# A mixture-of-experts layer on one core: bias rows packed in DRAM, a PSUM bank for each unit, the first pass written out, gathers by units

## The chip, the cores and the metric

The kernel runs on one core of one Trainium2 chip. The metric is the device time of one execution in microseconds. The kernel before takes 2048.38 us (median of three runs, 2045.47 to 2049.39). The execution that the profiler recorded took 2049.03 us; its span, from the first instruction to the last, is 2047.3 us.

Engines are called by their names in the profile: PE (TensorE), DVE (VectorE), ACT (ScalarE), POOL (GpSimd), SP (SyncE). An engine that ends in q (SPq, DVEq) is that engine's sequencer, which works through registers, branches and waits and issues the DMAs.

## The reference

One transformer-like layer on 1024 tokens of 1024 channels in float32: a modulated norm, a recurrent and a gated branch, an output projection, and then a mixture of 32 experts of which each token takes four. The part that the change touches is the experts:

```python
def expert_block(args):
    xb, e = args
    gu = xb @ w_gu[e] + b_gu[e]            # 1024 -> 2048
    g, lin = jnp.split(gu, 2, axis=-1)
    g = jnp.minimum(g, SWIGLU_LIMIT)
    lin = jnp.clip(lin, -SWIGLU_LIMIT, SWIGLU_LIMIT)
    act = g * jax.nn.sigmoid(SWIGLU_ALPHA * g) * (lin + 1.0)
    return act @ w_down[e] + b_down[e]     # 1024 -> 1024
...
ys = ys.astype(jnp.float32) * row_gate[:, None]
out = jnp.zeros((n_tok + 1, d), jnp.float32).at[row_tok].add(ys)[:n_tok]
```

An expert's weights are 12 MB (8 MB for `w_gu`, 4 MB for `w_down`), its biases 12 KB.

## The kernel before, in words

The program is written engine by engine, in order, with semaphores between them; nothing reorders it. The first 440 us compute the dense part, the routing and the tables. The rest is the experts.

**Units and items.** A unit is 32 rows (tokens) of one expert. The rows of an expert are cut into items of one to four units. This input has 47 items and 143 units. Experts are taken in an order of places: a large one, then a small one, and so on. A matrix product on PE has 32 rows as its stationary side, and four column quarters of the weights go through four 32-column tiles of the array. So the output of a unit lies in one PSUM bank as 128 partitions x 512 columns (gate and linear part) or x 256 (down).

**One item on PE** (`down_of`, `gate_and_linear_of`): the loop is turned by one stage. An iteration does the down product of item g (`down`, L1359, 64 matmul instructions a unit) and then the gate and linear product of item g + 1 (`gate_and_linear`, L1339, 64 a unit, in two halves of four weight slabs). Units are taken from the highest number to 0 (`units_down`), by branches on the item's count. Between the two stand small products that make the list of rows of a later item (`make_list`, L1299, `repeat_rows`, L1311). `down` writes banks 4 and 5 in turn, and for units 0 and 1 waits on `dn_drained` until DVE has read the result of two units before.

**The same item on DVE**: `block_rows` (one transpose of all gathered rows of the next item, L1942), the tables for the items after it (`make_onehot` L1934, `rows_here`, `make_idx`, `make_gates`, up to L1823), then for each unit `activate` (bias, limits, product with the sigmoid of ACT, transpose; L1969 to L1984), the list (`read_list` L1802), and for each unit `result` (down bias and gate weight; L1991, L1994). In front stand reads of words of the item's table into registers (L424). The loop body has this order for every item, the first one too.

**ACT** applies the norm's scale and shift to the transposed rows (`modulate`, L964) and the sigmoid (L974). **POOL** gathers the rows of an item by index (`gather`, L722; always four indirect DMAs, whatever the item's count) and adds results into an accumulator in DRAM (`scatter`, L733, one a unit). Both are 128 x 256 floats, in rows of 1 KB.

**SP** loads the weights in twelve chunks of 1 MB (L524). The buffers hold one expert, so chunk q of the next expert is issued when PE has used chunk q of this one for the last time (`freed[q]`). Between chunk 7 (the last of `w_gu`) and chunk 8 (the first of `w_down`) come the biases (`bias_in_rows`): eight DMAs, which copy the expert's biases to all 32 rows of each of four partition groups, in runs of 1 KB.

**The first item** has a pass of its own on PE (`first_1a` and so on), since its row tables are made at the same time; then the loops begin. SP, DVE, ACT and POOL enter their loops with item 0.

## Time and profile before

| | |
|---|---|
| median of three runs | 2048.38 us |
| the profiled execution, its span | 2049.03 us, 2047.3 us |
| PE busy | 1940.1 us, 95% of the span |
| DVE, POOL, ACT busy | 48%, 25%, 17% |
| DMA | 527.37 MB, 258 GB/s on average |
| mean granted TensorE clock | 0.983 |
| experts: PE's first gate product to its last down product | 445 to 2026 us |

Busy shares say which engine works most, not who waits for whom. The rows that follow the prediction's steps are in the section before it: each has its start in us from the span's start, its length, engine, source line, operation, and in square brackets the idle time of the engine before it and what ended it. The granted clock is in shares of 2.4 GHz: 1.00 is that level, 0.50 is 1.2 GHz, and a value between them is a stretch with both.

### The profile page before, as it was taken

Reading aid. Unit: us, or ns where it says so; the run is one execution under the profiler, and the core shown is the slowest. Engines: PE = TensorE matmul, PEld = TensorE weight load, DVE = VectorE, ACT = ScalarE, POOL = GpSimd, SP = SyncE. Lnnn points to the kernel's source line nnn. Section 1 sums busy time; section 2 is a strip of 40 time slices with the busy share of each in tenths; the row PEclk is TensorE's granted clock in tenths of the full one; section 3 lists DMA queues with packets and bytes.
Section 4 is the critical chain, followed back from the end, with each engine's and each line's share of the span. In section 5 each row is a group of like instructions: output and inputs, shape, how many; then the busy total and the mean of one; then the engine's idle time right before and its main releaser. Section 6 shows DMA issues by size and latency. Waiting matters only on the chain.

```text
span 2047.3 us, 53441 instructions
## 1 busy us (share of the span) xinstructions
PE 1940.1 (95%) x20292; PEld 812.1 (40%) x20293; DVE 989.9 (48%) x2301; ACT 356.0 (17%) x740; POOL 502.4 (25%) x540
## 2 busy tenths in 40 slices
PE   5999989968999999999999999999999999999996
PEld 3444444523333333334343443344334443334432
DVE  4666545354534445454444444454444454444435
ACT  4243121230100101111111111111111111111003
POOL 1100022133222222323232322323223222322221
PEclk9999999989999999999999999999999999999998
DMA  9333317341871964959595979879798898999995
GB/s 375 91 136 123 123 36 215 120 180 35 292 267 26 334 225 136 381 175 367 177 364 198 387 262 370 298 287 397 278 390 290 300 390 281 393 402 346 320 340 196
DMA packets 125697, 527.37 MB, mean 258 GB/s; under 512 B 17248, under 2 KB 47600, under 8 KB 75472
## 3 DMA queue, kind: packets, MB, share of 16 engines
q1 hardware_dynamic: 92272, 470.46, 58.9%
q0 software_dynamic: 33184, 56.29, 11.8%
q8 instruction: 20, 0.33, 0.1%
q14 instruction: 29, 0.24, 0.0%
q10 hardware_dynamic: 192, 0.06, 0.0%
HBM read 494.35 MB, written 32.38 MB: 257 GB/s over the span
## 4 chain that ended last, share of the span: by engine, by line
PE 81%; DMA 10%; DVE 3%; issue 2%; ACT 1%; SPq 1%; POOL 1%; DVEq 0%; another core or an unknown queue 0%; ACTq 0%; POOLq 0%
PE psum L1339 42%; PE psum L1359 20%; PE psum L1081 8%; DMA big<-in_exp_w_down_dram 6%; PE psum L1255 5%; DMA big<-in_exp_w_gu_dram 3%; PE psum L1192 2%; PE psum L1124 1%; PE psum L1299 0%; PE psum L1096 0%; SPq L524 0%; PE psum L1311 0%; DMA big<-in_w_out_dram 0%; PE psum L1106 0%
## 5 line engine op out<-in xcount | busy, mean ns | idle before, releaser
L1339 PE MATMUL psum<-big,r 128*32 128x512 f32 x9152 | 1001.8, 596 | 17.9 <-DMA big<-in_exp_w_gu_dram 9.0
L1339 PEld LDWEIGHTS psum<-big,r 128*32 128x32 f32 x9152 | 292.9, 110 | 680.0 <-issue 657.6
L1359 PE MATMUL psum<-big,r 128*32 128x256 f32 x9152 | 519.4, 383 | 25.6 <-DVE r L1984 16.9
L733 POOL DMA_INDIRECT acc_rows<-r,scatter_idx x139 | 220.5, 1586 | 778.6 <-DVE r L1994 746.5
L1359 PEld LDWEIGHTS psum<-big,r 128*32 128x32 f32 x9152 | 303.5, 111 | 220.9 <-DVE r L1984 22.7
L964 ACT ACTIVATE r<-r,shift 128x128 f32<-128x128 f32 x368 | 150.9, 480 | 883.2 <-PE psum L1339 698.4
L1969 DVE TENSOR_TENSOR r<-psum,r 128x256 f32<-128x256 f32 x143 | 59.1, 413 | 344.8 <-PE psum L1339 258.1
L722 POOL DMA_INDIRECT r<-hs_rows,gather_idx x188 | 185.8, 988 | 83.3 <-issue 43.1
L1991 DVE TENSOR_TENSOR r<-psum,r 128x256 f32<-128x256 f32 x143 | 60.7, 425 | 272.6 <-PE psum L1359 254.7
L1081 PE MATMUL psum<-r,big 128*128 128x512 f32 x384 | 166.3, 593 | 1.6 <-ACT r L853 1.6
L1942 DVE STREAM_TRANSPOSE r<-r 128x1024 f32<-128x1024 f32 x46 | 96.0, 2087 | 105.8 <-issue 105.8
L974 ACT ACTIVATE r<-r 128x256 f32<-128x256 f32 x143 | 59.6, 417 | 465.0 <-DVE r L1975 444.0
L1255 PE MATMUL psum<-big,r 128*128 128x512 f32 x256 | 112.2, 594 | 0.7 <-DMA big<-in_w_out_dram 0.5
L1081 PEld LDWEIGHTS psum<-r,big 128*128 128x128 f32 x384 | 72.6, 190 | 91.6 <-issue 89.2
L1984 DVE STREAM_TRANSPOSE r<-r 128x256 f32<-128x256 f32 x143 | 93.3, 653 | 4.9
L1980 DVE TENSOR_TENSOR r<-r 128x256 f32<-128x256 f32 x143 | 60.9, 426 | 49.9 <-ACT r L974 49.2
L1994 DVE SCALAR_TENSOR_TENSOR r<-r,g1row,g_rows 128x256 f32<-128x256 f32 x143 | 69.3, 485 | 5.1
L1255 PEld LDWEIGHTS psum<-big,r 128*128 128x128 f32 x256 | 47.8, 190 | 59.2 <-issue 57.8
L719 POOL COPY gather_idx<-r 128x4 int32 (+1 forms) x47 | 8.7, 186 | 249.8 <-DVE r L1816 249.8
L1934 DVE TENSOR_TENSOR r<-r 128x1024 bf16<-128x1024 f32 (+1 forms) x49 | 60.0, 1226 | 7.1 <-DVE r L1932 1.5
L1982 DVE TENSOR_TENSOR r<-r 128x256 f32<-128x256 f32 x143 | 60.8, 425 | 4.9
L1971 DVE SCALAR_TENSOR_TENSOR r<-psum,r 128x256 f32<-128x256 f32 x143 | 59.3, 415 | 0.0
(316 smaller groups left out, 938.4 us busy)
## 6 DMA issues: line engine op xcount, KB each, us to landing
big<-in_exp_w_gu_dram SPq DMA_DIRECT2D x256, 1024.0 KB
big<-in_exp_w_down_dram SPq DMA_DIRECT2D x128, 1024.0 KB
big<-in_ada_w_dram SPq DMA_DIRECT2D x12, 2048.0 KB, 13.8
r<-in_x_dram SPq DMA_DIRECT2D x16, 512.0 KB, 8.7
big<-in_w_in_dram SPq DMA_DIRECT2D x4, 2048.0 KB, 19.5
r<-in_exp_b_gu_dram SPq DMA_DIRECT2D x128, 64.0 KB
big<-in_w_out_dram SPq DMA_DIRECT2D x2, 2048.0 KB, 12.7
hs_rows<-r POOLq DMA_DIRECT2D x8, 512.0 KB, 3.0
```

Source lines behind the costliest of these rows:

```text
L722: pool.indirect_dma_start(z_quarters[:, u, :], None, hs_quarters, bass.IndirectOffsetOnAxis(ap=gather_idx[:, u:u + 1], axis=0)).then_inc(r ...
L733: pool.indirect_dma_start(acc_quarters, bass.IndirectOffsetOnAxis(ap=scatter_idx[:, u:u + 1], axis=0), y_sb[:, u, :], None, bounds_check=4 ...
L964: ins_ = act.activation(izT[:, k, :].rearrange("p (u n) -> p u n", u=UMAX), z_blocks[:, :, k, :], ACT.Identity, bias=shift2[:, 1, k:k + 1] ...
L1081: last = pe.matmul(b, w[:, k, m * P:(m + 1) * P], zT[:, k, th * 512:(th + 1) * 512], start=(k == 0), stop=(k == KT - 1))
L1255: last = pe.matmul(b, src[:, ct % CT, t * P:(t + 1) * P], ring(("wout", dh))[:, ct, :], start=(ct == 0), stop=(ct == 2 * CT - 1))
L1339: last = pe.matmul(psum[32 * j:32 * j + 32, u, :].rearrange("p (a n) -> p a n", a=2), izT[:, k, u * UNIT:(u + 1) * UNIT], rhs[:, :, 256 * ...
L1359: ins_ = pe.matmul(psum[32 * i:32 * i + 32, 4 + u % 2 if bank is None else bank, 0:256], actT[:, u, f, :], down_slab(f)[:, 256 * i:256 * i ...
L1942: dve.transpose(z_blocks, z_quarters.rearrange("p u (n k) -> p u k n", k=KT)).then_inc(z_blocked, 1)
L1980: dve.tensor_tensor(gsig_sb[:, u % 2, :], gate_u, sig_sb[:, u % 2, :], ALU.mult).then_inc(gsig_made, 1)
L1982: dve.tensor_tensor(act_sb[:, u % 2, :], lin_u, gsig_sb[:, u % 2, :], ALU.mult).then_inc(act_made, 1)
L1984: dve.transpose(actT[:, u, :, :], act_sb[:, u % 2, :].rearrange("p (n k) -> p k n", k=KT)).then_inc(at_made, 1)
L1994: dve.scalar_tensor_tensor(out=y_sb[:, u, :], in0=y_sb[:, u, :], scalar=gate_cur[:, u:u + 1], in1=g2_rows[:, :], op0=ALU.mult, op1=ALU.mul ...
```

## The change

It has four parts.

1. **Biases packed.** At the start POOL copies the biases of all experts with three DMAs from DRAM to DRAM into `bias_pack`, in which the 768 values that one partition group needs lie together. An expert's biases are then four DMAs with runs of 3 KB in place of eight with runs of 1 KB.
2. **A bank for each unit.** `down` writes bank 4 for unit 0 and bank u for unit u (the one that held its gate and linear part). Now the next item's gate product of unit u > 0 waits until that bank is drained (`results_of[u]`), unit 0's down product waits for all results of the item before, and PE computes four registers an item for that.
3. **The first pass written out.** Item 0 leaves the loops of DVE and ACT. DVE makes the table of item 3, activates item 0 and only then does `block_rows(1)` and the rest; ACT does item 0's sigmoids before it modulates item 1.
4. **Gathers by units.** POOL gathers only the units that an item has, and counts them in a register. DVE counts the same ahead of each `block_rows`: one more word read, up to three branches, up to four additions.

```diff
+            for a, (name, at) in enumerate((("exp_b_gu", 0), ("exp_b_gu", D), ("exp_b_down", 0))):
+                pool.dma_start(bias_pack[:, :, 256 * a:256 * a + 256],
+                               ins[name][0, :, at:at + D].rearrange("e (j n) -> e j n", j=4)).then_inc(bias_packed, SEMW)
...
                 for j in range(4):
-                    rows = bias_rows[32 * j:32 * j + 32, at:at + BIAS]
-                    sp_.dma_start(rows[:, 0:512].rearrange("p (a n) -> p a n", a=2),
-                                  ins["exp_b_gu"][0, bass.ds(e, 1), :].rearrange("o (a n) -> o a n", a=2)
-                                  [:, :, 256 * j:256 * j + 256].broadcast_to([UNIT, 2, 256])).then_inc(bias_in, SEMW)
-                    sp_.dma_start(rows[:, 512:768],
-                                  ins["exp_b_down"][0, bass.ds(e, 1), 256 * j:256 * j + 256].broadcast_to([UNIT, 256])
-                                  ).then_inc(bias_in, SEMW)
+                    sp_.dma_start(bias_rows[32 * j:32 * j + 32, at:at + BIAS],
+                                  bias_pack[bass.ds(e, 1), j, :].broadcast_to([UNIT, BIAS])).then_inc(bias_in, SEMW)
...
-                for u in range(UMAX):
-                    pool.indirect_dma_start(z_quarters[:, u, :], None, hs_quarters,
-                                            bass.IndirectOffsetOnAxis(ap=gather_idx[:, u:u + 1], axis=0)
-                                            ).then_inc(rows_in, SEMW)
+                units_down(pool, wanted, gather_unit)
...
+            units_down(act, act.to_reg(item_value(act, IT_UNITS, 0, 1, UMAX)), sigmoid)
+            act.wait_ge(freed[3], 1)
+            modulate(1, 0)
+            act.wait_ge(freed[7], 1)
+            modulate(1, 1)
             last_item = act.snap(total - 1)
-            with act.Fori(0, last_item) as g:
+            with act.Fori(1, last_item) as g:
...
+            def results_to_wait_for():
+
+                for u in range(UMAX):
+                    pe.reg_add(results_of[u], downs, SPARE - u)
...
+                    if k == 0 and u > 0 and steady:
+                        pe.wait_ge(dn_drained, results_of[u])
...
-                if u < 2 and bank is None:
-                    pe.wait_ge(dn_drained, downs)
+                if u == 0:
+                    pe.wait_ge(dn_drained, results_of[0])
...
-                        ins_ = pe.matmul(psum[32 * i:32 * i + 32, 4 + u % 2 if bank is None else bank, 0:256],
+                        ins_ = pe.matmul(psum[32 * i:32 * i + 32, DOWN_BANK[u], 0:256],
...
             with pe.Fori(0, last_item) as g:
                 down_of(g)
                 begin_item()
+                results_to_wait_for()
                 gate_and_linear_of(g + 1)
...
             def block_rows(turn):
 
-                dve.wait_ge(rows_in, turn * (UMAX * SEMW))
+                units_down(dve, dve.to_reg(item_value(dve, IT_UNITS, turn, 1, UMAX)),
+                           lambda u: dve.reg_add(rows_due, rows_due, SEMW))
+                dve.wait_ge(rows_in, rows_due)
...
-            with dve.Fori(0, last_item) as g:
+            make_onehot(3, link)
+            units, prior, place, bias_at = item_words(0)
+            activate_all(units, place, bias_at)
+            block_rows(1)
+            rows_here(4, link)
+            make_idx(2, link)
+            make_gates(2, link)
+            read_list(5)
+            link(dve.tensor_copy(gate_cur, gate_of[:, 0:UMAX]))
+            dve.wait_ge(acc_out, prior * SEMW + SEMW * TT)
+            dve.sem_inc(may_start, 1)
+            units_down(dve, units, lambda u: result(u, bias_at, DOWN_BANK[u]))
+            base = chain[0]
+            with dve.Fori(1, last_item) as g:
...
-                units_down(dve, units, lambda u: result(u, bias_at, 4 + u % 2))
+                units_down(dve, units, lambda u: result(u, bias_at, DOWN_BANK[u]))
```

What stands in DVE's program at the start of item 0, where the loop began before. TENSOR_LOAD at L424 is the read of a word of the item's table (L426 in the changed kernel), and L1942 the transpose of the next item's rows. Before:

```order
L2003 TENSOR_SCALAR r<-r 128x72
L2020 UNCONDITIONAL_BRANCH
L2020 ISA
L424 TENSOR_LOAD r
L424 ISA x3
L424 TENSOR_LOAD r
L424 ISA x3
L424 TENSOR_LOAD r
L424 ISA x2
L1939 ISA
L1942 STREAM_TRANSPOSE r<-r 128x1024
```

And in the changed kernel at the same place (L2029 is the old L2003, L1943 to L1956 make the table of item 3, L2042 is the wait for the biases):

```order
L2029 TENSOR_SCALAR r<-r 128x72
L426 TENSOR_LOAD r
L426 ISA x2
L426 TENSOR_LOAD r
L426 ISA x2
L1943 ISA
L1943 COPY g1row<-r 128x48
L1954 ISA
L1954 TENSOR_TENSOR r<-r 128x128
L1956 ISA
L1956 TENSOR_TENSOR r<-r 128x1024
L426 TENSOR_LOAD r
```

The transpose has gone from here, and with it one word read before the table; the transpose now follows the last unit's activation.

DVE in the loop of the changed kernel, after the fourth word read and ahead of the transpose (L1968, the old L1942); these rows are new:

```order
L433 COMPARE_AND_BRANCH
L433 UNCONDITIONAL_BRANCH
L433 COMPARE_AND_BRANCH
L433 UNCONDITIONAL_BRANCH
L433 COMPARE_AND_BRANCH
L433 UNCONDITIONAL_BRANCH
L1964 REGISTER_ALU
L435 UNCONDITIONAL_BRANCH
L1964 REGISTER_ALU
L435 UNCONDITIONAL_BRANCH
L1964 REGISTER_ALU
L435 UNCONDITIONAL_BRANCH
```

They are branches on the next item's count and additions to `rows_due`; they stand between the result of one item's unit 0 and the transpose.

## Rows read from the trace of the kernel before

**Rows 1.** The page's chain that ended last, by engine.
```profile
PE 81%; DMA 10%; DVE 3%; issue 2%; ACT 1%; SPq 1%; POOL 1%; DVEq 0%; another core or an unknown queue 0%; ACTq 0%; POOLq 0%
```
**Rows 2.** Waits of PE from 520 us on: in total, times, longest.
```profile
PE psum L1359 <- DVE r L1984: 11.8, 11, 4.9
PE psum L1339 <- DMA big<-in_exp_w_gu_dram: 9.0, 8, 2.7
...
PE psum L1359 <- DMA big<-in_exp_w_down_dram: 4.3, 6, 1.4
```
**Rows 3.** Timeline of PE, first item into second.
```profile
490.56 8.50 PE L1359 MATMUL psum<-big,r 128*32 128x256 f32 x128 [5.16 <-DVE r L1984]
501.10 7.11 PE L1359 MATMUL psum<-big,r 128*32 128x256 f32 x128 [2.04 <-issue]
508.14 0.25 PE L1311 MATMUL psum<-g1row,r 128*128 128x6 bf16 x4
508.33 7.07 PE L1339 MATMUL psum<-big,r 128*32 128x512 f32 x64
```
**Rows 4.** Timeline of DVE, first item.
```profile
481.22 2.07 DVE L1942 STREAM_TRANSPOSE r<-r 128x1024 f32<-128x1024 f32 x1 [2.52 <-issue]
...
483.69 1.22 DVE L1934 TENSOR_TENSOR r<-r 128x1024 bf16<-128x1024 f32 x1 [0.15 <-DVE r L1932]
...
487.44 0.42 DVE L1969 TENSOR_TENSOR r<-psum,r 128x256 f32<-128x256 f32 x1 [1.14 <-issue]
...
489.87 0.64 DVE L1984 STREAM_TRANSPOSE r<-r 128x256 f32<-128x256 f32 x1
...
498.76 0.65 DVE L1984 STREAM_TRANSPOSE r<-r 128x256 f32<-128x256 f32 x1
...
500.57 0.42 DVE L1991 TENSOR_TENSOR r<-psum,r 128x256 f32<-128x256 f32 x1 [1.05 <-issue]
```
**Rows 5.** Chain, first item: DVE's sequencer at word reads, then at branches.
```profile
478.92 0.32 DVEq L424
...
479.57 0.07 DVEq L424
...
486.54 0.08 DVEq L431
...
487.15 0.04 DVEq L1966
```
**Rows 6.** PE in a stretch: length, busy, granted clock, DMA share, GB/s.
```profile
490.00:495.00 5.00, 4.44 (x56) 0.66 0.31 84
```
**Rows 7.** Timeline of PE: the longest weight stall at each of three experts.
```profile
1174.60 7.93 PE L1339 MATMUL psum<-big,r 128*32 128x512 f32 x72 [1.79 <-issue]
...
1266.89 9.63 PE L1339 MATMUL psum<-big,r 128*32 128x512 f32 x72 [2.72 <-DMA big<-in_exp_w_gu_dram]
...
1453.43 7.98 PE L1359 MATMUL psum<-big,r 128*32 128x256 f32 x144 [1.37 <-DMA big<-in_exp_w_down_dram]
```
**Rows 8.** DMA queues at 691.9:694.5, then 469:480: packets, MB, share of 16 engines.
```profile
q1 hardware_dynamic: 537, 0.47, 60.5%
...
q0 software_dynamic: 192, 0.52, 15.9%
```
**Rows 9.** A stretch with weights alone: length, POOL busy, clock, DMA share, GB/s.
```profile
973.00:978.00 5.00, 0.00 (x0) 1.00 1.02 405
```
**Rows 10.** Timeline of SP: first bias issue of an expert, and first w_down issue.
```profile
1245.00 0.34 SPq L531 DMA_DIRECT2D r<-in_exp_b_gu_dram  x1
...
1250.09 9.92 SPq L524 DMA_DIRECT2D big<-in_exp_w_down_dram  x4
```
**Rows 11.** Timeline of DVE in a two-unit item.
```profile
1049.11 0.16 DVE L1823 TENSOR_TENSOR r<-g1row 128x4 f32 x1
1051.48 0.43 DVE L1969 TENSOR_TENSOR r<-psum,r 128x256 f32<-128x256 f32 x1 [2.20 <-PE psum L1339]
```
**Rows 12.** Timeline of PE: unit 0's down product in the same item.
```profile
1059.42 3.66 PE L1359 MATMUL psum<-big,r 128*32 128x256 f32 x64 [0.18 <-DVE r L1984]
```

More of the change, by code:

```diff
@@ L70 @@
 BIAS = 768
+BIAS_LOADS = 4
 LISTS = MAX_ITEMS + 3
@@ L567, in _ @@
                     if q == 7:
-                        sp_.wait_ge(bias_in, SEMW * 8 * place)
+                        sp_.wait_ge(bias_in, SEMW * BIAS_LOADS * place)
                         if place >= 2:
@@ L1321, in _ @@
             downs = counter(pe, "downs")
-            all_drained = pe.alloc_register("all_drained")
+            results_of = [counter(pe, f"results_of{u}") for u in range(UMAX)]
+            def results_to_wait_for():
+                for u in range(UMAX):
+                    pe.reg_add(results_of[u], downs, SPARE - u)
+            results_to_wait_for()
             def load_word(turn, i):
@@ L1331, in begin_item, with gate_and_linear @@
                 pe.reg_add(arrived, arrived, SEMW)
-            def gate_and_linear(u, half, first=False, between=None):
+            def gate_and_linear(u, half, first=False, between=None, steady=False):
                 for k in range(4 * half, 4 * half + 4):
@@ L1347, in gate_and_linear, with down @@
                     last.then_inc(gu_made, 1)
-            def down(u, bank=None):
+            def down(u, last=False):
                 pe.reg_add(downs, downs, 1)
                 pe.wait_ge(at_made, downs)
-                if u < 2 and bank is None:
-                    pe.wait_ge(dn_drained, downs)
+                if u == 0:
+                    pe.wait_ge(dn_drained, results_of[0])
                 for f in range(KT):
@@ L1358, in down @@
                     for i in range(4):
-                        ins_ = pe.matmul(psum[32 * i:32 * i + 32, 4 + u % 2 if bank is None else bank, 0:256],
+                        ins_ = pe.matmul(psum[32 * i:32 * i + 32, DOWN_BANK[u], 0:256],
                                          actT[:, u, f, :], down_slab(f)[:, 256 * i:256 * i + 256],
                                          start=(f == 0), stop=(f == KT - 1), skip_group_check=True)
-                    if u == 0 and f in (1, 3, 5) and bank is None:
+                    if u == 0 and f in (1, 3, 5) and not last:
                         ins_.then_inc(freed[8 + f // 2], 1)
@@ L1442, in gate_and_linear_of @@
                 pe.wait_ge(z_made[0], g + 1)
-                units_down(pe, units, lambda u: gate_and_linear(u, 0))
+                units_down(pe, units, lambda u: gate_and_linear(u, 0, steady=True))
                 pe.wait_ge(z_made[1], g + 1)
@@ L1466, in _ @@
             spread = counter(pe, "spread")
-            pe.reg_add(all_drained, downs, SPARE)
-            pe.wait_ge(dn_drained, all_drained)
-            units_down(pe, units, lambda u: down(u, DOWN_BANK[u]))
+            units_down(pe, units, lambda u: down(u, last=True))
             units_down(pe, units, spread_sum)
@@ L2049, in last_step @@
                 ins_.then_inc(dve_chain, 1)
-                dve.wait_ge(dve_chain, loops + (base + count_[0]))
+                dve.wait_ge(dve_chain, loops + (base - STEPS + count_[0]))
             units, prior, place, bias_at = item_words(last_item)
```

21 lines of the change are left out of this document (16 added, 5 removed).

## The prediction, as recorded before the changed kernel ran

> **What bounds the kernel now.** I read the chain that ended last, then PE's waits, then timelines where PE stands still. PE holds 81% of the chain and DMA 10% [rows 1]. So time can be won only where PE waits, or be lost where PE gets a new wait. From 520 us on PE waits little: 11.8 us for DVE, 9.0 and 4.3 us for weights [rows 2]; with 1.8 us that the profile calls issue in the middle of a gate product [rows 7] the weight stalls are 15.1 us. In a four-unit item nothing is left to win: the small list product is followed by the next gate product with no idle time [rows 3]. The largest single hole lies in the first item. PE waits 5.16 us for DVE, runs two units' down products in 8.50 us, waits another 2.04 us, and runs the other two in 7.11 us [rows 3]. The second wait is the bank: unit 1 needs unit 3's result, and DVE does that result, at 500.57, only after all four activations [rows 4]. The first two units are slower by 1.4 us since the granted clock is 0.66 after the wait, a mix of 2.4 and 1.2 GHz, against 1.00 later [rows 6].
>
> **First pass and banks.** Before, DVE reads three words, transposes item 1's rows for 2.07 us from 481.22, reads two more words, makes the table of item 3 (1.22 us from 483.69) and starts to activate at 487.44 [rows 4]. A word costs 0.65 us, the time between two reads in the chain, and the first read begins at 478.92 [rows 5]. After, in steps:
> - two reads end at 480.2; the table starts 0.4 us later, as it did behind the transpose, and is done at 481.8;
> - three reads run beside it and end near 482.7; three branches take 0.61 us (486.54 to 487.15 [rows 5]) and the first instruction comes 0.3 us after them [rows 4]: activation starts at 483.6, its transpose ends 3.1 us later (487.44 to 490.51 [rows 4]), at 486.7;
> - PE starts unit 3's down product at about 486.8 in place of 490.56. Units are activated every 2.96 us (489.87 to 498.76 for three [rows 4]), a down product takes 3.5 us, so it then never waits. I let the clock fall again, as it did after the wait of 5.16 us, and keep the 1.4 us. End of four units: 486.8 + 14.1 + 1.4 = 502.3;
> - with a bank per unit the 2.04 us wait goes. What is late next is the first gate product of item 1, which now wants unit 3's result. DVE: last activation ends 495.6, one read and the branches and additions 1.6, transpose 2.07, tables 1.6 (484.91 to 486.54 [rows 4, 5]), list and copy 0.2, on to the result 1.05 + 0.42 [rows 4], so 502.6. ACT needs 1.65 us behind the transpose (499.3) and is earlier.
> So item 1 starts at about 502.8 and not 508.33 [rows 3]: -5.5 us. Bounds: -3.7 if only the start moves and another wait takes the place of the 2.04; -7.2 if clock and result cost nothing. In the other items the bank change removes nothing, as no wait on it shows in PE's list, and adds a wait only on results that are several units old.
>
> **Weight stalls.** They come where a small item, or an item that is an expert's only one, gives the next 12 MB too little time. By the unit counts of the timeline (matmul count over 64) there are eight such places. Their stalls: 1.7 at 572 us, 2.7 at 720, 1.0 at 852, 4.1 at 1162 to 1188, 3.4 at 1254 to 1267, 1.7 at 1451 to 1453, 0.2 and 0.4 later (the longest of three of them in [rows 7]). There the DMA engines are full, so what counts is their time. An expert's biases are 384 KB in 1 KB runs. In the stretch where they dominate SP's queue, 0.47 MB take 60.5% of 2.6 us, 1.57 us [rows 8], so 0.39 MB take 1.31 us; at the weights' 405 GB/s [rows 9] they would take 0.97. Packed: -0.34 us an expert. Bounds: 0, and the whole 1.31. A gather that isn't made saves 15.9% of 11 us over four, 0.44 us [rows 8]. Before the stalls at 1162, 1254 and 1451 three unit gathers go (items of two and three units ahead): 0.34 + 3 x 0.44 = 1.66 each, 5.0 together. The biases lie behind the `w_gu` chunks in SP's order, so the first three stalls gain only by gathers: none, one (0.44), none. The last two, 0.6, vanish. Sum -6.1 us. Gathers and packing elsewhere are worth nothing.
>
> The Trainium skill (DMA: Bandwidth & Descriptors, section Bandwidth) says that transfers under 64 KB are bound by their descriptors and gives 0.95 us of DMA time for 64 KB. By that, eight pieces against four would be worth some 2.6 us an expert, an estimate from that page, and the sum would be about 4 us lower; the 1.57 us for all of 0.47 MB in this trace speaks against it.
>
> **What the loops gain in work.** DVE's count of gathered rows stands between the last result and the transpose, where DVE is idle for the sequencer already: a read 0.65, three branches 0.61 [rows 5], additions and jumps about 0.3 at 0.04 to 0.1 each (L1966 [rows 5]): 1.6 us an item, estimated. Behind it on DVE wait the table and all activations, and PE waits for these. In items of three and four units DVE idles several us before the first activation. In the 11 two-unit items it idles 2.20 us, of which 1.0 is its branches [rows 11, 4]: cover 1.2, so the activation is 0.4 late. PE waits 0.18 us at unit 0 already [rows 12], so 0.22 us an item; three of them run into a weight stall that hides it: 8 x 0.22 = +1.8 us. The two one-unit items pay the full 1.6 (PE's 4.9 us wait [rows 2] becomes 6.5), but the stalls of 1.7 and 2.7 us behind them take it up: 0. Bounds: 0 to 11 x 1.6 = 18. I stay near the low end because the cover is a row.
>
> The Trainium skill (Advanced Engine Details and Errata, Control Flow Timing) gives about 108 ns for a compare-and-branch and 51 ns for a plain branch. By these the activation would be hardly late and the sum 1.8 us lower; the trace has 0.20 us for each of three branches on DVE, and goes first.
>
> POOL's branches are hidden, since POOL (25% busy) waits for DVE ahead of every scatter. The packing runs some 200 us before the first bias is wanted, so SP's wait for it is long met. PE's four register additions and its waits stand at a place where four register operations and three branches leave no gap [rows 3]: 0.
>
> **Sum.** -5.5 - 6.1 + 1.8 = -9.8 us. The profiled execution took 2049.03 us (span 2047.3, 1.7 around it), 0.65 above the median of the runs. 2049.0 - 9.8 = 2039.2 us.
>
> **Rivals.**
> - *A, the stalls stay.* The weights alone need 12.6 MB / 405 GB/s = 31 us an expert, and a three-unit item lasts 31.7. If the engines lose the saved time elsewhere, only the first pass counts: -5.5 + 1.8, 2045.3 us. For it: the chain's DMA pieces of 24 to 27 us. Against: gathers show a plain share of engine time.
> - *B, SP's issues are the limit.* Bias issues fill 5.09 us ahead of `w_down` [rows 10]; halved, `w_down` starts 2.5 us sooner. With 1.3 for gathers that clears up to 3.9 at 1162, and 3.4 and 1.7 whole, with 0.44 and 0.6: -10.0, so 2035.3 us. Against: the engines are full in that stretch, so an earlier issue only queues.
> - *C, the first pass gains little*, as a late word read or code fetch on DVE holds it: -1.5, with the rest 2043.2 us. The 1.05 and 1.14 us gaps [rows 4] show how dear DVE's sequencer is.
> - *D, slower.* PE's sequencer has no lead at the item boundary, and four additions, 0.09 us each on DVE with the gap before them [rows 5], stand open: 0.36 x 46 = +16.6 us, 2055.8 us. It is slower than before from 0.21 us an item. Against: the gap between L1311 and L1339 is zero now [rows 3].
>
> **Chances.** Forecast 0.55, A 0.17, B 0.12, C 0.07, D 0.09. Range 2032 to 2050 us: it takes in A, B, C and the bounds of the first pass, and half of the open cost on DVE, and leaves out D. A measurement tells 0.2% (4.1 us) from no change, so faster means below 2044.3: forecast and B nearly whole, most of C, a third of A: 0.76. Same 0.14. Slower 0.10.
>
> **What would show it.** First unit's down product near 486.8 and item 1's first gate product near 502.8, with no wait between units 2 and 1. Weight stalls of about 9 us in place of 15.1. DVE's idle time before the block transpose up from 2.3 to about 3.9 us; PE's wait at unit 0 of two-unit items up from 0.18 to about 0.4. No gap between L1311 and the next gate product. I am wrong if that gap opens, if two-unit items lose more than 0.5 us, or if the stalls are as long as before.

## The result, and the profile after

The changed kernel takes 2027.74 us (median of 4 runs, 2026.08 to 2030.74), the kernel before 2046.93 (median of 4, one run more than above). The ratio is 0.9911, 95% interval 0.9895 to 0.9927: 18 to 19 us faster, where 9.8 us were forecast. The direction was right; the forecast gain is about half of the measured one, and the time lies below the forecast's range of 2032 to 2050 us.

PE's waits of the changed kernel from 520 us on (in total, times, longest):

```profile
PE psum L1362 <- DMA big<-in_exp_w_gu_dram: 10.2, 8, 2.2
PE psum L1382 <- DVE r L2010: 9.8, 2, 4.9
PE psum L1487 <- ACT r L1034: 6.4, 4, 3.9
PE psum L1313 <- DVE r L1956: 3.3, 2, 1.7
PE psum L1382 <- DMA big<-in_exp_w_down_dram: 3.3, 5, 1.4
```

Beside [rows 2] this is a riddle: 13.5 us for weights, against 15.1 before, and the kernel is 18 us faster. The first item, timeline of PE (start, length, operation, idle time before):

```profile
486.59 0.22 PE L1421 MATMUL psum<-ident_b 128*1 128x8 bf16 x3
486.74 0.35 PE L1313 MATMUL psum<-g1row,r 128*128 128x6 bf16 x8
490.37 15.71 PE L1382 MATMUL psum<-big,r 128*32 128x256 f32 x256 [3.28 <-DVE r L2010]
506.01 0.25 PE L1325 MATMUL psum<-g1row,r 128*128 128x6 bf16 x4
506.20 6.22 PE L1362 MATMUL psum<-big,r 128*32 128x512 f32 x56
```

A repeat product is the small product of `repeat_rows` (L1311 before, L1325 now) that closes an item's down products; the signals are the three small products at L1421 (L1398 before), right behind the first pass. Everything up to the signals lies 3.8 us later in this execution, and of the change only the packing of the biases has run by then. The last repeat product ahead of the signals began between 479 and 486 us in the profiles of all kernels here, with packing and without it, in no order, so distances count. From the three signals (L1421) to item 1's first gate product it is 19.61 us, against 25.51 before (482.82 to 508.33, [rows 3]): -5.9, forecast -5.5. The wait between units 2 and 1 is gone, and the gate product follows the repeat product without a gap, so rival D falls.

Then a two-unit item. The first two fences are PE in the kernel before, and DVE in the same place; the third is PE in the changed kernel:

```profile
840.55 0.35 PE L1299 MATMUL psum<-g1row,r 128*128 128x6 bf16 x8
840.84 0.64 PE L1359 MATMUL psum<-big,r 128*32 128x256 f32 x8
841.76 3.28 PE L1359 MATMUL psum<-big,r 128*32 128x256 f32 x56 [0.28 <-issue]
845.23 3.66 PE L1359 MATMUL psum<-big,r 128*32 128x256 f32 x64 [0.19 <-DVE r L1984]
848.82 0.26 PE L1311 MATMUL psum<-g1row,r 128*128 128x6 bf16 x4
```

```profile
840.00 0.65 DVE L1984 STREAM_TRANSPOSE r<-r 128x256 f32<-128x256 f32 x1
842.09 0.42 DVE L1969 TENSOR_TENSOR r<-psum,r 128x256 f32<-128x256 f32 x1 [1.43 <-PE psum L1339]
```

```profile
834.52 0.35 PE L1313 MATMUL psum<-g1row,r 128*128 128x6 bf16 x8
834.81 7.11 PE L1382 MATMUL psum<-big,r 128*32 128x256 f32 x128
841.85 0.26 PE L1325 MATMUL psum<-g1row,r 128*128 128x6 bf16 x4
```

In this execution of the kernel before, PE had finished unit 0's gate product by about 840.6 us and DVE was free too, but DVE began on it only at 842.09, after 1.4 us of idle time. The item took some 1.0 us more, and so it was in all eleven two-unit items: 11.5 us. I call it the hole. It looks like the missing half of the gain, since the changed kernel's profile has none. It isn't, as the experiments show.

### The profile page after: what moved, and what is told of

The parts are those of the page before. It is cut to its first block, busy times and chain, and to the rows that moved or that the text cites. A ratio compares the mean times of both kernels' runs of the same rounds, so it can differ in the third digit from the quotient of the medians.

```text
span 2028.9 us, 54052 instructions
## 1 busy us (share of the span) xinstructions
PE 1929.8 (95%) x20292; PEld 802.2 (40%) x20293; DVE 993.3 (49%) x2301; ACT 356.2 (18%) x740; POOL 463.3 (23%) x498
## 4 chain that ended last, share of the span: by engine, by line
PE 85%; DMA 10%; DVE 2%; ACT 1%; issue 1%; POOL 1%; DVEq 0%; ACTq 0%; SPq 0%; POOLq 0%
PE psum L1362 42%; PE psum L1382 23%; PE psum L1095 8%; DMA big<-in_exp_w_down_dram 6%; PE psum L1269 5%; DMA big<-in_exp_w_gu_dram 3%; PE psum L1206 2%; PE psum L1138 1%; PE psum L1313 1%; PE psum L1110 0%; PE psum L1325 0%; DVE r L2114 0%; DMA big<-in_w_out_dram 0%; PE psum L1120 0%; PE psum L1224 0%
## 5 line engine op out<-in xcount | busy, mean ns | idle before, releaser
L1362 PEld LDWEIGHTS psum<-big,r 128*32 128x32 f32 x9152 | 291.6, 110 | 677.2 <-issue 652.9
L1382 PE MATMUL psum<-big,r 128*32 128x256 f32 x9152 | 509.9, 382 | 16.3 <-DVE r L2010 13.1
L1382 PEld LDWEIGHTS psum<-big,r 128*32 128x32 f32 x9152 | 293.7, 111 | 211.9 <-DVE r L2010 13.3
L1968 DVE STREAM_TRANSPOSE r<-r 128x1024 f32<-128x1024 f32 x46 | 95.9, 2086 | 170.6 <-issue 170.6
L731 POOL DMA_INDIRECT r<-hs_rows,gather_idx x143 | 142.7, 998 | 123.6 <-issue 123.6
L1956 DVE TENSOR_TENSOR r<-r 128x1024 bf16<-128x1024 f32 (+1 forms) x49 | 60.0, 1225 | 7.1 <-DVE r L1954 0.9
## 6 DMA issues: line engine op xcount, KB each, us to landing
big<-in_exp_w_gu_dram SPq DMA_DIRECT2D x256, 1024.0 KB, 11.7
```

Source lines behind the costliest of these rows:

```text
L731: pool.indirect_dma_start(z_quarters[:, u, :], None, hs_quarters, bass.IndirectOffsetOnAxis(ap=gather_idx[:, u:u + 1], axis=0)).then_inc(r ...
L1362: last = pe.matmul(psum[32 * j:32 * j + 32, u, :].rearrange("p (a n) -> p a n", a=2), izT[:, k, u * UNIT:(u + 1) * UNIT], rhs[:, :, 256 * ...
L1382: ins_ = pe.matmul(psum[32 * i:32 * i + 32, DOWN_BANK[u], 0:256], actT[:, u, f, :], down_slab(f)[:, 256 * i:256 * i + 256], start=(f == 0) ...
L1968: dve.transpose(z_blocks, z_quarters.rearrange("p u (n k) -> p u k n", k=KT)).then_inc(z_blocked, 1)
```

## The experiments

Each ratio is against the kernel before on the same chip; the groups of runs came from several chips, so kernels of different groups are best compared by their ratios. Beside the times I use one measure: the time from one item's repeat product to the next is 42.03, 31.71 or 21.39 us for an item of four, three or two units where nothing waits; what is above that is the item's stall. The first item is counted from the last repeat product ahead of the signals. The three stall columns start at 842 us; the one-unit items at 550 and 697 us and the items behind them are not in them. The profile shows one execution and the time is the median of several, so the two need not agree (the profiled execution of "banks, first pass" was the slowest of its eleven). Each run gave one profile, so a row's stalls scatter by some 2 us, at 1150 and 1240 us by more.

| kernel | median us | ratio (95%) | first item | stalls at 842 | 1150 and 1240 | from 1300 |
|---|---|---|---|---|---|---|
| before, three profiles | 2045 to 2047 | 1 | 29.0, 28.8, 28.8 | 1.2, 1.9, 1.2 | 10.7, 11.0, 15.7 | 3.4 (with 11.5 of holes), 10.4, 9.8 |
| banks only | 2043.9 | 0.9991 (0.9981 to 1.0002) | 26.8 | 1.3 | 13.1 | 10.0 |
| first pass only | 2047.5 | 1.0004 (0.9994 to 1.0014) | 29.9 | 3.1 | 11.0 | 10.5 |
| banks, first pass | 2041.8 | 0.9974 (0.9963 to 0.9986) | 23.0 | 3.0 | 14.0 | 11.8 |
| changed, one wait more | 2029.0 | 0.9912 (0.9899 to 0.9925) | 23.0 | 1.7 | 10.6 | 2.2 |
| changed, down(1) in bank 5 | 2026.7 | 0.9905 (0.9890 to 0.9919) | 23.0 | 2.0 | 9.6 | 0.0 |
| packed biases only | 2043.2 | 0.9991 (0.9983 to 1.0000) | 28.8 | 2.1 | 12.2 | 5.8 |
| gathers by units only | 2038.9 | 0.9968 (0.9955 to 0.9980) | 30.7 | 2.3 | 11.2 | 3.9 |
| packed, gathers | 2037.7 | 0.9952 (0.9939 to 0.9966) | 30.7 | 1.8 | 11.8 | 2.4 |
| changed, gathers back | 2037.8 | 0.9964 (0.9952 to 0.9977) | 23.0 | 3.0 | 11.7 | 7.4 |
| changed, biases back | 2030.2 | 0.9922 (0.9909 to 0.9935) | 23.1 | 2.0 | 9.8 | 3.3 |
| changed, two profiles | 2027.7 | 0.9911 (0.9895 to 0.9927) | 23.1, 23.1 | 2.4, 1.9 | 10.7, 8.5 | 1.4, 1.0 |
| changed, biases ahead, two buffers | 2037.3 | 0.9963 (0.9949 to 0.9977) | 23.0 | 5.9 | 8.9 | 0.4 |
| changed, biases ahead, three buffers | 2039.5 | 0.9971 (0.9958 to 0.9983) | 23.1 | 6.3 | 7.9 | 0.1 |
| before, made hole | 2048.7 | 1.0014 (1.0006 to 1.0023) | 28.7 | 1.6 | 8.3 | 0.4 |
| changed, made hole | 2040.4 | 0.9975 (0.9965 to 0.9985) | 23.1 | 0.0 | 6.2 | 0.0 |
| changed, no bias loads | 2019.2 | 0.9874 (0.9859 to 0.9889) | 23.1 | 0.8 | 1.0 | 0.1 |

**1. Banks only.**

```
-        SPARE = 2
+        SPARE = 3
...
+                    if k == 0 and u > 0 and steady:
+                        pe.wait_ge(dn_drained, results_of[u])
...
-                if u < 2 and bank is None:
-                    pe.wait_ge(dn_drained, downs)
+                if u == 0:
+                    pe.wait_ge(dn_drained, results_of[0])
...
+                        ins_ = pe.matmul(psum[32 * i:32 * i + 32, DOWN_BANK[u], 0:256],
```

> The kernel before with one part of the change: a bank of its own for each unit's down product, and with it TensorE's waits on dn_drained moved (before at down(1) and down(0), now at gate(1..3) of the next item and at down(0)). Theory W (in the eleven two-unit items the first down product carries the wait on dn_drained before, and that is why DVE sees gu_made of unit 0 some 1.2 us late and down(0) starts late; the bank part alone removes it): 0.93 us x 11 = 10 us less, some of it given back to later weights, 2037 to 2040; the rows of a two-unit item show down x128 in one piece and DVE's first step of unit 0 right behind the transpose of unit 1. Rival G (the four gathers on GpSimd at that moment delay the signal, so it is the gathers by units that removed it): no change, 2045 to 2048, and the row with 1.43 us of idle time on DVE stays. The prediction on record gave this part 0.

No change clear of noise (0.9991, 0.9981 to 1.0002). The hole was gone, as theory W wants, and the gathers were not touched, against rival G. But the time, 2043.9 us, didn't follow into W's 2037 to 2040. Runs 8 and 12 below show that the kernel before mostly has no hole either, so its absence here decides neither.

**2 and 3. One wait more at down(1); down(1) in bank 5.** In the changed kernel:

```
-                if u == 0:
-                    pe.wait_ge(dn_drained, results_of[0])
+                if u == 0 or u == 1 and not last:
+                    pe.wait_ge(dn_drained, results_of[u])
```

> The changed kernel with one wait more: down(1) of every item also waits on dn_drained, for a count that gate(1) has waited for already, so that it never has to wait; banks as changed. Theory W (the instruction with the wait is what delays): the loss of the two-unit items comes back, 8 to 10 us, 2036 to 2038, with DVE idle 1.4 us before its first step of unit 0. Rival P (the PSUM bank: before, down(1) wrote bank 5, now bank 1): nothing comes back, 2027 to 2029.

```
-        DOWN_BANK = (4, 1, 2, 3)
-        SUM_BANK = (5, 6, 7, 0)
+        DOWN_BANK = (4, 5, 2, 3)
+        SUM_BANK = (1, 6, 7, 0)
```

> The changed kernel with down(1) in bank 5, as before, and the waits as changed. Rival P: the two-unit items lose their 0.93 us again, 2036 to 2038. Theory W: 2027 to 2029, and down x128 in one piece.

2029.0 us (0.9912, 0.9899 to 0.9925) and 2026.7 (0.9905, 0.9890 to 0.9919), two-unit items of 21.40 us in both. Neither the wait nor the bank brought the hole back, against W and P; with runs 8 and 12, where the kernel before has both the wait and the bank and no hole, neither is enough to make it.

**4. First pass only.** ACT's and DVE's share of item 0 ahead of their loops, activation first:

```
+            make_onehot(3, link)
+            units, prior, place, bias_at = item_words(0)
+            activate_all(units, place, bias_at)
+            block_rows(1)
...
-            with dve.Fori(0, last_item) as g:
+            with dve.Fori(1, last_item) as g:
```

> The kernel before with one part of the change: the first pass of DVE and ACT written out (activation of item 0 ahead of the block transpose, modulation ahead of the loop). By the prediction's first term the gate product of item 1 starts 5.5 us nearer to the first signal (25.5 us before, some 19.6 now): 2041 to 2042. If later weight stalls swallow a part, 2043 to 2044; the stalls from 1150 to 1270 us then grow by that.

No gain at all, and a miss of mine. PE in that kernel's first item:

```profile
487.73 8.80 PE L1364 MATMUL psum<-big,r 128*32 128x256 f32 x128 [3.23 <-DVE r L1989]
501.51 8.80 PE L1364 MATMUL psum<-big,r 128*32 128x256 f32 x128 [4.98 <-issue]
```

The first wait is 3.23 in place of 5.16 us [rows 3], but units 1 and 0 now wait 4.98 us in place of 2.04. The profile names no releaser for that wait; by the program it is their bank, since the results that free it stand behind block transpose and tables as before, and run 9 bears this out: with a bank for each unit the wait is gone. The first item is 1.1 us longer.

**5 to 7. Packed biases only; gathers by units only; both.**

```
-                    rows = bias_rows[32 * j:32 * j + 32, at:at + BIAS]
-                    sp_.dma_start(rows[:, 0:512].rearrange("p (a n) -> p a n", a=2),
...
-                    sp_.dma_start(rows[:, 512:768],
...
+                    sp_.dma_start(bias_rows[32 * j:32 * j + 32, at:at + BIAS],
+                                  bias_pack[bass.ds(e, 1), j, :].broadcast_to([UNIT, BIAS])).then_inc(bias_in, SEMW)
...
+            for a, (name, at) in enumerate((("exp_b_gu", 0), ("exp_b_gu", D), ("exp_b_down", 0))):
+                pool.dma_start(bias_pack[:, :, 256 * a:256 * a + 256],
...
```

> The kernel before with the biases packed in DRAM and loaded in four pieces, and nothing else of the change. The two runs with the bank part and the first pass part alone changed no time: both lost the 0.93 us hole of the two-unit items and paid it back in weight stalls (20.5 and 21.6 us against 15.1). Theory S (from 1150 us on the weights' arrival sets the time, and the eight bias DMAs between chunk 7 and chunk 8 are what holds it up): the stalls fall to 2 to 6 us, and the time to 2031 to 2038, lowest if the hole in the two-unit items goes as well. Theory of the record (packing is worth 0.34 us an expert, at the stalled experts alone): 2045 to 2046. Rival T (it is the gathers that hold the weights up): 2045 to 2048.

```
-                for u in range(UMAX):
-                    pool.indirect_dma_start(z_quarters[:, u, :], None, hs_quarters,
...
+                units_down(pool, wanted, gather_unit)
...
-                dve.wait_ge(rows_in, turn * (UMAX * SEMW))
+                units_down(dve, dve.to_reg(item_value(dve, IT_UNITS, turn, 1, UMAX)),
+                           lambda u: dve.reg_add(rows_due, rows_due, SEMW))
+                dve.wait_ge(rows_in, rows_due)
```

> The kernel before with gathers for the units of an item only, and DVE's count of them, and nothing else. Theory of the record: up to 5 us less stall at 1162 to 1454 us, 1.8 us more on DVE in two-unit items, so 2043 to 2045. Theory S: the stalls hardly change, 2045 to 2049. Rival T: 2034 to 2040.

> The kernel before with packed biases and gathers by units, without the banks and without the written-out first pass. Theory S: the supply is now free, what is left to the other two parts is the first pass, 5 to 6 us of the 19: 2032 to 2034. If the parts simply add, it is 2028, since banks and first pass alone gave nothing.

By the ratios, packing alone gave 1.8 us, at the edge of noise (theory S, which wanted 8 or more from it, falls in this form; the other two had 2045 or more, and it was 2043.2); the gathers alone 6.5, which only T had in its range; both 9.8 (2037.7 us, where S had 2032 to 2034 and the plain sum 2028, so both were missed). In the table the last column goes from 10 us to 5.8, 3.9 and 2.4. The gathers also have a price: DVE's count makes the first item 1.95 us longer, open on the path.

**8 and 12. The kernel before again, unchanged.**

> The kernel before, unchanged, for a second profile. If the hole of 0.28 us in the down product and DVE's 1.4 us before the last activation in two-unit items belong to the program (where its code lies, say), they are in this profile as well, 22.3 to 22.7 us for such an item; if they belong to one execution, the items take 21.4 us here.

> The kernel before, unchanged, a third profile, for how often the hole of the two-unit items comes: 22.4 us an item if it is there, 21.4 if not. The time should be some 5 us higher with it.

The hole is in neither: 21.39 us for each of the 22 two-unit items. They took 2043.54 and 2047.73 us, the execution with the holes 2049.03. So it belongs to an execution. The one-unit items at 550 and 697 us with their successors took 128.9 us in the execution with the holes and 125.4 and 125.0 in the other two, which is in no column of the table. PE's waits from 520 us on in the second one:

```profile
PE psum L1339 <- DMA big<-in_exp_w_gu_dram: 14.0, 10, 2.4
...
PE psum L1359 <- DMA big<-in_exp_w_down_dram: 8.9, 8, 1.4
```

22.9 us for weights, where the profile shown had 15.1. One of the late stalls in it, where the execution shown has a short wait only:

```profile
1681.22 0.25 PE L1311 MATMUL psum<-g1row,r 128*128 128x6 bf16 x4
1681.40 13.08 PE L1339 MATMUL psum<-big,r 128*32 128x512 f32 x120
1694.87 7.93 PE L1339 MATMUL psum<-big,r 128*32 128x512 f32 x72 [0.38 <-DMA big<-in_exp_w_gu_dram]
1702.74 0.35 PE L1299 MATMUL psum<-g1row,r 128*128 128x6 bf16 x8
1703.02 1.93 PE L1359 MATMUL psum<-big,r 128*32 128x256 f32 x32
1705.44 1.07 PE L1359 MATMUL psum<-big,r 128*32 128x256 f32 x16 [0.48 <-DMA big<-in_exp_w_down_dram]
1707.87 7.98 PE L1359 MATMUL psum<-big,r 128*32 128x256 f32 x144 [1.36 <-DMA big<-in_exp_w_down_dram]
1715.78 0.26 PE L1311 MATMUL psum<-g1row,r 128*128 128x6 bf16 x4
```

From 1681.22 to 1715.78 it is 34.56 us, 2.85 over 31.71. There are five such items from 1300 us on. Each is the first item of an expert whose weights are loaded during the only item, of three units, of the expert before it; at 1150 and 1240 us that only item has two units.

**9. Banks and first pass together** (the diffs of 1 and 4).

> The kernel before with the banks and the written-out first pass together, biases and gathers as before. Apart they took 2.0 us out of the first item (28.75 to 26.75 us from one repeat product to the next) and put 1.1 us in (29.89). Theory I (they work only together: a unit activated early waits for the bank, a free bank waits for the activation): some 22.9 to 23.1 us here, 5.8 less, and nothing of it lost later, since a weight stall is local to its expert: 2039 to 2042. Theory S' (the weights' arrival holds the end fixed, so any time won ahead of 1150 us goes into stalls): 2044 to 2047, with stalls 4 to 6 us longer.

Theory I holds for the first item, 23.0 us, and for the time, 5.3 us faster (0.9974, so 2.9 to 7.6) and outside the range of S'. But in this one profile, of the slowest of eleven executions, the three stall columns have 28.8 us, 3.8 more than the mean of the second and third profile before, where S' had 4 to 6. So that nothing is lost later is not shown.

**10 and 13. Biases an expert ahead.** Their DMAs behind the last `w_down` chunk of the expert before, with two buffers and with three:

```
...
-                    if q == 7:
...
-                        bias_in_rows(e, place)
+                if place + 1 < NE:
+                    bias_ahead(place + 1)
```

> The changed kernel with the bias DMAs of the next expert issued behind the last w_down chunk, an expert ahead, in place of between chunk 7 and chunk 8. Theory D (the DMA engines' time is what the stalled experts lack: the 0.39 MB leave the full stretch, some 1 us at each of eight stalls, where biases of the next expert take their place only in a stretch that is not full): 3 to 7 us less stall, 2021 to 2025. Theory Q (SP's issues, 2 us of them ahead of w_down, are what is lacking): the wait for w_down, 3.3 us in 5, goes and the wait for w_gu stays, 2024 to 2026. If neither: 2027 to 2029.

> The changed kernel with the biases an expert ahead, as in the run before, but with a third buffer for them, so that SP doesn't wait for the results of the expert just finished. With two buffers the late stalls (from 1300 us) were 0.3 us in place of 1.4 and the wait for w_down 0.6 in place of 3.3, but w_gu waits of 1.3 to 5.9 us came at 845, 957 and 1064 us. If SP standing at dn_drained ahead of chunk 0 made these: they go, 2022 to 2026. If the four bias issues and the word reads ahead of chunk 0 are enough to make them (some 3 us): 2032 to 2038 again.

Both slower than the changed kernel: 2037.3 us (0.9963, 0.9949 to 0.9977) and 2039.5 (0.9971, 0.9958 to 0.9983). The third buffer didn't help, so SP's wait for results is not the cause. In both the stalls from 1300 us are nearly gone (0.4 us with two buffers), but that at 842 us grew from 2.4 to 5.9 and 6.3, and four-unit items near 955 and 1062 us, which never waited, wait 0.9 to 1.8 us. PE at 842 us with three buffers:

```profile
844.93 1.07 PE L1368 MATMUL psum<-big,r 128*32 128x512 f32 x8 [0.62 <-DMA big<-in_exp_w_gu_dram]
847.22 1.90 PE L1368 MATMUL psum<-big,r 128*32 128x512 f32 x8 [1.22 <-DMA big<-in_exp_w_gu_dram]
850.27 20.13 PE L1368 MATMUL psum<-big,r 128*32 128x512 f32 x168 [1.15 <-DMA big<-in_exp_w_gu_dram]
```

The bias loads now lie ahead of `w_gu`, which PE wants first. With two buffers the profiled execution is 7.1 us longer than that of the changed kernel, and the items account for 6.8 of it: 3.3 us more at the one-unit items and behind them, 3.5 at 842 us, 2.8 near 955 and 1062, less 1.8 at 1150 and 1240 and 1.0 from 1300. Why a load there costs so much more than between chunk 7 and chunk 8 was not settled.

**11 and 15. The changed kernel with the gathers back, or with the biases back.**

> The changed kernel with all four gathers for every item again, and so without DVE's count: banks, first pass and packed biases stay. From the gathers part alone (2038.9 against 2045.7, stalls behind 5.9 us shorter, first item 1.95 us longer): with the first pass written out its count costs nothing there, so it should be worth more here: 2034 to 2036 without it. If parts add as ratios: 2034.

> The changed kernel with the biases in eight DMAs with rows of 1 KB again: banks, first pass and gathers by units stay. From bias packing alone (1.8 us) and on top of the gathers (3.3 us): 2030 to 2032 without it. The forecast's price of 0.34 us at the stalled experts: 2028.5 to 2029.5. Late stalls up from 1.4 to 3 or 4 us.

2037.8 and 2030.2 us: on top of the other parts the gathers are worth 10 us (the ratios say 11) and packing 2.4. The intervals of the ratios with and without packing overlap (0.9895 to 0.9927 and 0.9909 to 0.9935), so packing's share of the time is not clear of noise; the late stalls, 3.3 us without it and 1.4 and 1.0 with it, point the same way. The gathers' range was missed, they are worth more than I wrote.

**14 and 17. A hole made on purpose, in the kernel before and in the changed one.**

```
+            def hole():
+
+                pe.wait_ge(w_arrived[8], arrived)
+                for i in range(2):
+                    for j in range(4):
+                        pe.matmul(psum[32 * j:32 * j + 32, 3, :], down_slab(1)[:, 0:UNIT], down_slab(0)[:, 0:512],
+                                  start=True, stop=True, skip_group_check=True)
...
```

(in two-unit items only, ahead of down(1); bank 5 in the changed kernel)

> The kernel before, with eight matrix products of 128 x 512 (0.88 us) that nothing needs, ahead of the down products of each two-unit item: the hole that one of three profiles of it had, made on purpose, 11 x 0.9 = 9.7 us of TensorE. Theory S (the weights set the pace in the last part: a hole there only shortens the stall behind it): late stalls 10 us to 3 or 4, and the time only 1 to 4 us up, 2046 to 2049. Theory PE (TensorE's time adds to the end): 2054 to 2056.

> The changed kernel with the same useless products as in the run before last group's hole: eight in the program, which the trace of that run shows as sixteen of 1.74 us together, in each of eleven two-unit items, 19 us of TensorE in all. In the kernel before they cost 3 us. Theory S: the changed kernel has 1.3 us of late stalls left and 11 to 14 at three places further ahead (842, 1150, 1240 us), each behind one two-unit item, so it can hide 1.3 + 3 x 1.7 = 6 us of the 19: 2039 to 2042. If the changed kernel still were held by the weights: 2029 to 2032.

In the kernel before (L1453 is the hole):

```profile
1301.28 0.35 PE L1299 MATMUL psum<-g1row,r 128*128 128x6 bf16 x8
1301.57 1.92 PE L1453 MATMUL psum<-big 128*32 128x512 f32 x16
1303.31 7.09 PE L1359 MATMUL psum<-big,r 128*32 128x256 f32 x128
```

The eight products came out as sixteen, 1.74 us (1301.57 to 1303.31), twice what I had meant: 19 us of TensorE in all. They cost 2.9 us (1.0014, 1.0006 to 1.0023), within theory S and far from theory PE, which with 19 us would have had some 2065. The stalls from 1300 us fell from 10 to 0.4, those at 1150 and 1240 to 8.3. In the changed kernel the same products cost 12.7 us (2040.4 us), inside the range that was expected. The three stall columns fell to 6.2 us, from 14.5 and 11.4. Its waits for weights were then:

```profile
PE psum L1362 <- DMA big<-in_exp_w_gu_dram: 4.3, 4, 1.7
...
PE psum L1382 <- DMA big<-in_exp_w_down_dram: 2.3, 2, 1.3
```

**16. The changed kernel again.**

> The changed kernel, unchanged, for a second profile: its late stalls 0 to 2.5 us, those at 1150 and 1240 us 9 to 11 us together, as in its first profile and its two near copies, against 10 us and 11 to 16 us in the second and third profile of the kernel before.

2027.81 us, stalls 1.9, 8.5 and 1.0. A little under the range at 1150 and 1240.

**18. The changed kernel without bias loads from the third expert on** (it leaves out this part of the computation; its sums use stale biases).

```
-                        bias_in_rows(e, place)
+                        if place < 2:
+                            bias_in_rows(e, place)
+                        else:
+                            sp_.sem_inc(bias_in, SEMW * BIAS_LOADS)
```

> The changed kernel without the bias loads from the third expert on (the sums then use stale biases, so this part of the computation is left out): 29 x 0.39 MB that the DMA engines don't move and 4 issues less an expert on SP. Theory D (engine time, 1 us an expert, in the full stretches): late stalls 1.3 to 0, those at 842, 1150 and 1240 us 3 us shorter together, 2023 to 2025. Theory O (what counts in the queue is only what lies ahead of w_gu, and the biases lie behind it): only the wait for w_down goes, 3 us, 2024 to 2026. If biases are free where they are: 2027 to 2028.

2019.2 us: 8.5 less than the changed kernel (7.6 by the ratios), beyond all three theories. The loads' bytes and SP's four issues go together here, so the run doesn't say which of the two counts. The wait for `w_down` is gone and that for `w_gu` down to 2.9 us:

```profile
PE psum L1365 <- DMA big<-in_exp_w_gu_dram: 2.9, 4, 1.0
```

## Why the prediction was right and wrong

- *First pass and banks, -5.5.* Right in size and nearly in all its steps. From the signals to the first down product I had 4.0 us and it was 3.78; four units took 15.71 us where I had 15.5 with the 1.4 us of slow clock kept, and the granted clock from 490 to 495 us was 0.66 again; item 1's gate product came 0.4 us sooner than forecast. I had it wait for DVE's result of unit 3; that result was done at 505.24, and PE's own work at 506.2 was what came last. With biases and gathers as before, the two parts give 5.3 us. What I didn't say: neither gives anything clear of noise alone (runs 1 and 4).
- *Gathers and packing, "Sum -6.1 us".* This is the step that failed, in the sentences "The last two, 0.6, vanish" and "Gathers and packing elsewhere are worth nothing". I took as the most that could be won the stalls of one execution, 15.1 us, of which some 3 lay behind 1300 us. Two other executions of the same program have 10 there, at five items, and the changed kernel 1.4 and 1.0. In the table's three stall columns the kernel before has 23 and 27 us in these two, the changed kernel 14.5 and 11.4: -12 in place of -6.1. By place: from 1300 us on -8.9, where I had -2.3 (0.6 and 1.7); at 1150 and 1240 us -3.8, where I had -3.3; at 842 us +0.6. The price was right: 1.66 us at each of five items would have been 8.3 (an estimate), and runs 11 and 15 put 6.2 us of it on the gathers and 2.1 on packing, where my prices for five items make 6.6 and 1.7. What was wrong is the number of places: of these five stalls the profile that I read showed one of 2.1 us and 1.3 us in the other four together, so there seemed to be nothing to win there. (The recorded sum is also 0.1 too high: 5.0, 0.44 and 0.6 are 6.0, which makes the forecast 2039.3.) I expected some 9 us in PE's waits for weights; they were 13.5 and, in the second profile, 10.6, against 22.9 and 23.3 in the two executions without the hole. A likely reason why the first execution differs comes from run 14: a hole in TensorE's work ahead of a stall gives the weights more time, and the stall shortens by it. 19 us of made holes took 15 us of stalls away (25 in the mean of the second and third profile, 10.3 with the hole), and the 11.5 us of the first execution's own go with 10 us less stall. That made holes and stalls trade in this way is shown; that the first execution's own holes did the same fits its numbers and is argued from them. What made the hole in one execution of three is open.
- *DVE's count, +1.8.* The first half of the mechanism was there, the second not. DVE's idle time before the block transpose went from 2.3 us to 3.7 in the mean, where I had 3.9. In the first item it cost 1.95 us where nothing hid it (run 6), and none in the written-out first pass. In two-unit items it cost nothing: 21.40 us against 21.39. The first activation, unit 1's, does start later, by 0.26 us (11.20 us behind the repeat product in place of 10.94), where I had 0.4. But unit 0's starts where it did, 14.36 us behind the repeat product, because before it waited 0.20 us for its own gate product, and PE never stands still. PE's 0.18 us at unit 0 [rows 12], from which I carried the delay on, belongs to the execution with the hole; without the hole down products of both units run in one piece. The two activations in the kernel before (second profile), then in the changed one:

```profile
835.49 0.42 DVE L1969 TENSOR_TENSOR r<-psum,r 128x256 f32<-128x256 f32 x1 [2.31 <-PE psum L1339]
838.91 0.42 DVE L1969 TENSOR_TENSOR r<-psum,r 128x256 f32<-128x256 f32 x1 [0.20 <-PE psum L1339]
```

```profile
831.67 0.42 DVE L1995 TENSOR_TENSOR r<-psum,r 128x256 f32<-128x256 f32 x1 [1.04 <-PE psum L1362]
834.83 0.42 DVE L1995 TENSOR_TENSOR r<-psum,r 128x256 f32<-128x256 f32 x1
```

In the two one-unit items the count was absorbed by the stall behind, as written (it shows as waits of up to 1.7 us ahead of the list product, L1313, and not, as I had it, as a longer wait of 4.9 us at the down product): both items with their successors took 125.4 and 125.0 us before (second and third profile), 125.0 after. The Trainium skill (Advanced Engine Details and Errata, Control Flow Timing) gives about 108 ns for a compare-and-branch and 51 ns for a plain branch. What I worked out from it, no cost in two-unit items, came nearer to this result, but for another reason. Each of the three branches is a compare-and-branch with a plain branch behind it; by the page that is 0.16 us, an estimate, and the trace has 0.20. What hid the delay was that unit 0's activation waited for its own product.

- *"In the other items the bank change removes nothing".* Right, once the hole is known not to be the bank's (runs 1 to 3, 8, 12).
- *Rivals.* A falls with the late stalls. B gave the lowest time, 2035.3, and was still too high; whether SP's issues or the engines' time are what packing saves, no run separates (runs 10 and 13 moved the loads to a place where they cost more, run 18 took away both). The full engines in the stretch shown below speak for their time. C falls by the first item, D by the missing gap.
- *Sum.* -5.7 (first item, 28.8 to 23.1) - 12 (stalls) + 0 (DVE's count) = -18, and 18 to 19 were measured.
- *The price of a bias load.* I took 1.31 us an expert unpacked and 0.97 packed. The changed kernel microsecond by microsecond (stretch, length, granted clock, DMA share, GB/s), where two gathers and a bias load fall into a full stretch:

```profile
1163.00:1164.00 1.00, 1.00 1.02 432
1164.00:1165.00 1.00, 1.00 1.04 313
1165.00:1166.00 1.00, 1.00 0.97 233
1166.00:1167.00 1.00, 1.00 1.18 261
1167.00:1168.00 1.00, 1.00 0.91 268
1168.00:1169.00 1.00, 1.00 1.03 401
```

The engines are as full as ever and from 1164 us on move 1.08 MB in 4 us, where weights alone make 1.6 at 405 GB/s [rows 9]. Of these 0.39 MB are bias and 0.26 gathers, so weights have 0.43, 1.0 us' worth: 3.0 us for the rest, less two gathers at 0.44 [rows 8], 2.1 us for the bias, an estimate. Run 18 agrees: with two experts' biases gone, the stretch from the first `w_gu` issue at 1105.5 us (1102.6 there) to the end of the stalled item is 4.1 us shorter. The Trainium skill (DMA: Bandwidth & Descriptors, section Bandwidth) holds transfers under 64 KB to be bound by their descriptors, which made eight DMAs against four worth some 2.6 us an expert, an estimate; packing was worth 2.4 us in the whole kernel, so in this the trace disagrees. The packed loads are 96 KB each, above the page's 64, and by the estimate still cost more than the 0.97 us of their bytes.

## What to carry to other kernels

A stall in one execution's profile is no measure of what a faster supply can win. Where the busiest engine and the transfers are nearly level, holes in the engine's work hide stalls behind them (19 us of them took 15 us of stall away here), so add the holes to the stalls, or take a second profile. The cheapest test of which of the two sets the time is a useless piece of work on the engine: 19 us of it cost 3 us before the change and 12.7 after. And parts that each change nothing clear of noise can be worth 5 us together, where one releases what the other waits for.

## What the runs showed of the hardware that I had not expected

- Eight float32 products of 32 rows by 512 columns in the program (the made hole) appear in the trace as sixteen and take 1.74 us. The needed ones show the same doubling: a unit's gate product is 32 in the program and 64 in the trace.
- The hole: in one execution of three, at the same place of all eleven two-unit items, DVE began on a finished product 15.6 to 16.0 us behind the repeat product, where it is 14.4 in the others: 1.2 to 1.6 us late. None of nineteen other profiles of this kernel and its variants has it.
- 12 KB of biases, spread to 128 partitions by DMA, cost the DMA engines about 2 us by the estimate above, as long as 0.8 MB of weights. Without them the kernel is 8.5 us faster. A cheaper way to spread them was not tried.
